# The first modulation and the LRU input in sixteen blocks of features, with fp32 products and a ring of 17 weight places

## What is computed

```python
c_act = silu(c)
mod = c_act @ w_ada + b_ada                      # 6 * 2048 columns
shift1, scale1, gate1, shift2, scale2, gate2 = split(mod, 6)
h = rms_norm(x, norm1_g) * (1 + scale1) + shift1
proj = h @ w_in                                  # 10752 columns
lru_x, lru_gate, q, k, v, g_a, g_b = split(proj)
xc = causal_depthwise_conv(lru_x, conv_w, conv_b)    # 4 taps along the sequence
# r, i = sigmoid(xc @ 128x128 blocks); rec = scan along the sequence of (a, u)
# y_a = (rec * gelu(lru_gate)) @ w_lru_out; y_b = attention(q, k, v) @ w_attn_out
```

## Time and profile before

| what | us |
|---|---|
| median of 3 runs (2783.32 to 2784.49) | 2783.36 |
| the profiled execution, its time | 2785.63 |
| its span | 2783.8 |
| TensorE busy in the span | 2671.4 (96%) |
| VectorE busy | 1963.2 (71%) |
| ScalarE busy | 1458.5 (52%) |

### The profile page before, as it was taken

The page is one execution under the profiler, slowest core; times in us unless marked ns, Lnnn a source line. Parts: engine busy times, 40 slices in busy tenths (PEclk is TensorE's granted clock), DMA queues, the critical chain, the costliest instruction groups (busy, mean ns, idle before and its releaser), DMA issues.

```text
span 2783.8 us, 40811 instructions
## 1 busy us (share of the span) xinstructions
PE 2671.4 (96%) x16090; PEld 2356.3 (85%) x16090; DVE 1963.2 (71%) x2783; ACT 1458.5 (52%) x2183; POOL 141.1 (5%) x177
## 2 busy tenths in 40 slices
PE   4789899999999999999999999999999999999996
PEld 4778788888888788888888888888988888889885
DVE  7985788887898866666566676666566766664666
ACT  3356666655545555555555545545555455445543
POOL 0000000000001000000000010100001221000002
PEclk8899999999999999999999999999999999999998
DMA  8965677778889775655566555665545556655452
GB/s 331 376 223 166 200 243 253 261 262 280 289 303 328 255 251 183 187 192 190 187 183 197 188 178 166 189 178 175 158 148 187 187 173 183 181 182 155 144 178 102
DMA packets 162110, 584.12 MB, mean 210 GB/s; under 512 B 19040, under 2 KB 20320, under 8 KB 161792
## 3 DMA queue, kind: packets, MB, share of 16 engines
q1 hardware_dynamic: 157104, 566.86, 62.7%
q0 software_dynamic: 4528, 12.43, 1.6%
q10 hardware_dynamic: 288, 2.23, 0.2%
HBM read 574.05 MB, written 2.15 MB: 207 GB/s over the span
## 4 chain that ended last, share of the span: by engine, by line
PE 86%; DVE 10%; ACT 2%; issue 1%; DMA 0%; SPq 0%; ACTq 0%; DVEq 0%
PE bank L726 49%; PE bank L734 25%; DVE raw L1408 3%; DVE wlo L1367 3%; PE bank L699 2%; PE bank L701 2%; PE bank L700 2%; PE pO L783 1%; PE pS L760 1%; PE pT L772 1%; DVE XC L1824 1%; PE pS L813 1%; ACT whi L977 1%; DMA CR<-in_c 0%; DVE bank L1810 0%
## 5 line engine op out<-in xcount | busy, mean ns | idle before, releaser
L1367 DVE TENSOR_TENSOR wlo<-raw,whi 128x1024 fp32r<-128x1024 f32 (+1 forms) x880 | 1075.2, 1234 | 460.4 <-ACT whi L977 456.7
L977 ACT ACTIVATE whi<-raw 128x1024 fp32r<-128x1024 f32 (+1 forms) x880 | 912.2, 1048 | 446.4 <-PE bank L734 355.2
L726 PE MATMUL bank<-H,whi 128*128 128x512 f32 x4000 | 1020.6, 397 | 4.7 <-DVE H L1675 3.7
L726 PEld LDWEIGHTS bank<-H,whi 128*128 128x128 f32 x4000 | 723.8, 190 | 147.0 <-issue 6.3
L734 PEld LDWEIGHTS bank<-H,wlo 128*128 128x128 f32 x4000 | 547.7, 191 | 43.4 <-DVE wlo L1367 4.1
L734 PE MATMUL bank<-H,wlo 128*128 128x256 f32 x4000 | 560.2, 283 | 2.1 <-DVE wlo L1367 2.1
L726 PE MATMUL bank<-F,whi 128*128 128x512 f32 x1024 | 256.4, 392 | 0.0
L1408 DVE SCALAR_TENSOR_TENSOR raw<-raw,CR 128x1024 f32<-128x1024 f32 x192 | 230.7, 1217 | 0.0
L726 PEld LDWEIGHTS bank<-F,whi 128*128 128x128 f32 x1024 | 184.3, 189 | 32.8
L1197 ACT ACTIVATE ET<-bank 128x512 f32<-128x512 f32 x116 | 69.1, 596 | 193.8 <-PE bank L734 193.8
L1810 DVE TENSOR_TENSOR bank<-bank,ET 128x512 f32<-128x512 f32 x116 | 80.9, 698 | 96.2 <-ACT ET L1197 96.2
(11 more groups left out here) (305 smaller groups left out, 2955.7 us busy)
## 6 DMA issues: line engine op xcount, KB each, us to landing
raw<-in_w_in SPq DMA_DIRECT2D x424, 512.0 KB, 4.2
raw<-in_w_ff SPq DMA_DIRECT2D x256, 512.0 KB, 4.3
raw<-in_ada SPq DMA_DIRECT2D x192, 512.0 KB, 5.2
raw<-in_w_out SPq DMA_DIRECT2D x96, 512.0 KB, 4.7
raw<-in_w_lru_out SPq DMA_DIRECT2D x32, 512.0 KB, 4.6
raw<-in_w_attn_out SPq DMA_DIRECT2D x32, 512.0 KB, 4.9
raw<-in_w_kv SPq DMA_DIRECT2D x32, 512.0 KB, 4.6
BT<-gtab POOLq DMA_DIRECT2D x32, 128.0 KB, 4.3
```

The source lines that it names most:

```text
L726: pe.matmul(out[i].rearrange("p (a s) -> p a s", a=2), whi[:, s, at_:at_ + 128], both[:, :, kt, :], start=(c == 0 and k == 0), stop=False, ...
L977: act.activation(whi[:, s, 0:el.n], raw[el.slot][:, 0:el.n], ACT.Copy).then_inc(s_hi, 1)
L1367: dve.tensor_tensor(wlo[:, s, 0:n], raw[el.slot][:, 0:n], v32(whi[:, s, 0:n]), ALU.subtract).then_inc(s_lo, 1)
```

## The change

- The LRU stage goes block by block of the input features: 16 steps b, each with the four ada chunks of its own 128 columns of scale1 and shift1 and two weight chunks. A weight chunk ("w32") is now one block of input features by 1024 output columns and isn't split: TensorE multiplies it as fp32, straight from `raw`, by the fp32 `XR` block (`products_plain`, 8 matmuls of 256 columns); the place comes free when TensorE is done with it. Half 0 goes to banks 0 to 3, half 1 to banks 4 to 7.
- ScalarE modulates in place once for each block; H in its two parts, which later units need, is made of four blocks at a time (one copy on ScalarE, one subtraction on VectorE, `low1`).
- The ring has 17 places in this stage (0 to 4 and 6 to 17; eight new ones lie where AT and XC come later). The last two weight chunks are bound to places 6 to 9, the next ones to 0 to 4.
- The convolutions run behind the last products: two at once, the other six as side work (`convs`), one each two ticks, spread over unit q0 to q2. Gates begin after q2, two sets go beside unit q4, and the last two beside k.
- `c` comes in two loads from two queues, x in four pieces behind c, the constants and `vec`; most of `decay` is put off to step b = 6.

```diff
-NRAW = 10
+NRAW = 18
...
-    for q in range(4):
-        mark("norm1", q)
-        for j in range(8):
-            unit("lrux", j, "in", j, "H1", nkc=1, corder=(q,), part=("open", "more", "more", "close")[q])
-            if (q, j) == (3, 0):
-                steps.append(("ring", (0, 1, 2, 3, 4)))
+    for b in range(NB):
+        mark("norm1", b)
+        for half in range(2):
+            unit("lrux", half, "x", half, "H1", nkc=1, corder=(b,), part="open" if b == 0 else "close" if b == NB - 1 else "more")
     mark("lru_weights")
     for j in range(8):
-        unit("q", j, "in", 8 + j, "H1")
-        if j == 0:
+        unit("q", j, "in", j, "H1")
+        if j == 2:
             mark("bias")
-        if j < 7:
-            mark("gates", j)
-        if j == 6:
-            mark("gates", 7)
-    unit("k", 0, "in", 16, "H1")
+            mark("gates", 0)
+        elif j == 3:
+            mark("gates", 1)
+            mark("gates", 2)
+        elif j > 3:
+            mark("gates", j - 1)
+    mark("gates", 7)
+    unit("k", 0, "in", 8, "H1")
     mark("scan")
-    unit("v", 0, "in", 17, "H1", mode="t")
+    unit("v", 0, "in", 9, "H1", mode="t")
...
...
     first_end = []
...
+    def columns(block):
+        for half in range(2):
+            modulation(block, half)
...
-        stream.append(Elem("w", 4 * un.width, (un.src, un.u, un.kc0 + un.corder[c]), ord=len(order) - 1))
...
+        stream.append(Elem("w32" if un.part else "w", CH if un.part else 4 * un.width, (un.src, un.u, un.kc0 + un.corder[c]),
+                           ord=len(order) - 1))
...
+    columns(16)
+    columns(0)
+    first_end.append(len(stream) - 1)
+    for b in range(1, NB):
+        weight(parts[2 * b - 2], 0)
+        columns(16 + b)
+        weight(parts[2 * b - 1], 0)
+        columns(b)
+        first_end.append(len(stream) - 1)
+    rings.append((len(stream), (6, 7, 8, 9)))
+    weight(parts[-2], 0)
+    weight(parts[-1], 0)
+    rings.append((len(stream), (0, 1, 2, 3, 4)))
...
+        if el.kind == "w32":
+            done.append(("chunk", el.ord + 1))
+            continue
...
-            un.bank = un.j
+            un.bank = 4 * un.j
...
-        if un.part in ("", "close"):
+        if un.part == "close" and un.j == 0:
+            holder = {0: ("lrux", 2), 1: ("lrux", 4)}
...
+    raw += [at(f"raw{10 + i}", [128, CH], o_a + i * 4096) for i in range(8)]
...
-        sp.dma_start(vec[:, :], d_vec).then_inc(s_vec, 16)
-        for h in range(2):
-            sp.dma_start(CR[h][:, :], d_c[:, h * CH:(h + 1) * CH]).then_inc(s_c, 16)
+        sp.dma_start(CR[0][:, :], d_c[:, 0:CH]).then_inc(s_c, 16)
...
+        def products_plain(un):
+            ch = un.chunks[0]
+            el = stream[order[ch]]
+            kt = un.corder[0]
+            pe.wait_ge(s_hf, kt + 1)
+            pe.wait_ge(s_raw[el.slot], el.landed)
+            for k in range(8):
+                ins = pe.matmul(banks[un.bank + k // 2][:, k % 2 * 256:k % 2 * 256 + 256], raw[el.slot][:, k * 128:(k + 1) * 128],
+                                XR[:, kt, :], start=(un.part == "open" and k % 2 == 0), stop=(un.part == "close" and k % 2 == 1),
+                                skip_group_check=True)
+            ins.then_inc(s_mm, 1)
...
+                elif un.kind == "q" and un.j == 0:
+                    pe.wait_ge(*ready["H1"](kt))
...
-                act.activation(Hhi[:, b, :], XR[:, b, :], ACT.Identity, scale=A1v[:, b:b + 1],
-                               bias=mod[:, b:b + 1]).then_inc(s_hh, 1)
-                if b >= 4:
-                    act.wait_ge(s_h, b - 3)
-                act.activation(tslot(b), XR[:, b, :], ACT.Identity, scale=A1v[:, b:b + 1],
-                               bias=mod[:, b:b + 1]).then_inc(s_slp, 1)
+        def norm1(b):
+            act.wait_ge(s_mod, b + 1)
+            act.wait_ge(s_xr, b // 2 + 1)
+            act.activation(XR[:, b, :], XR[:, b, :], ACT.Identity, scale=A1v[:, b:b + 1], bias=mod[:, b:b + 1]).then_inc(s_hf, 1)
+            if b % 4 == 3:
+                act.wait_ge(s_hf, b + 1)
+                act.activation(Hhi[:, b - 3:b + 1, :], XR[:, b - 3:b + 1, :], ACT.Copy).then_inc(s_hh, 4)
...
+        def conv(j):
+            if j == 0:
+                for r in range(14, 18):
+                    act.wait_ge(*last_use[r])
+            act.wait_ge(s_mm, first_split - 1 + j // 4)
+            for i in range(2):
+                b = 2 * j + i
+                ins = act.activation(XC[:, b, :], banks[j][:, i * 256:(i + 1) * 256], ACT.Identity, scale=v(V_CW + 48 + b),
+                                     bias=v(V_CB + b))
+            ins.then_inc(s_pre, 1)
+        def convs():
+            conv(2)
+            yield
+            for j in range(3, 8):
+                conv(j)
+                yield from ticks(2)
...
+            if kind == "q":
+                if j == 0:
+                    for r in range(10, 14):
+                        act.wait_ge(*last_use[r])
...
+        act.dma_start(CR[1][:, :], d_c[:, CH:2 * CH]).then_inc(s_c, 16)
         act.dma_start(cst[:, 0:C_DUP], d_cst[:, 0:C_DUP]).then_inc(s_cst, 16)
-        act.dma_start(RES[:, :, :], d_x).then_inc(s_x, 16)
+        act.dma_start(vec[:, :], d_vec).then_inc(s_vec, 16)
+        for q in range(4):
+            act.dma_start(RES[:, 4 * q:4 * q + 4, :], d_x[:, 4 * q:4 * q + 4, :]).then_inc(s_x[q], 16)
...
-        act.wait_ge(s_x, 16)
         for j in range(8):
+            act.wait_ge(s_x[j // 2], 16)
...
-                    side.start(gates(st[2], 3 if st[2] == 7 else 1))
...
-            evac(un)
+            if un.part:
+                if un.j == 0:
+                    conv(0)
+                    conv(1)
+                else:
+                    side.start(convs())
+            else:
+                evac(un)
...
-        def first_columns(q):
-            sums(first_end[q])
-            both = [slice(16 + 4 * q, 20 + 4 * q), slice(4 * q, 4 * q + 4)]
-            for c in both:
-                t = vc.add(dve.tensor_tensor(mod[:, c], mod[:, c], mod2[:, c], ALU.add))
+        def first_columns(b):
+            sums(first_end[b])
+            for c in (16 + b, b):
+                t = vc.add(dve.scalar_tensor_tensor(out=mod[:, c:c + 1], in0=mod[:, c:c + 1], scalar=mod2[:, c:c + 1],
+                                                    in1=v(V_ADA + c), op0=ALU.add, op1=ALU.add))
             dve.wait_ge(s_vc, t)
-            for c in both:
-                t = vc.add(dve.tensor_tensor(mod[:, c], mod[:, c], vec[:, V_ADA + c.start:V_ADA + c.stop], ALU.add))
-            dve.wait_ge(s_vc, t)
-            dve.scalar_tensor_tensor(out=A1v[:, 4 * q:4 * q + 4], in0=mod[:, both[0]], scalar=1.0, in1=v(V_N1 + 4 * q, 4),
+            dve.scalar_tensor_tensor(out=A1v[:, b:b + 1], in0=mod[:, 16 + b:17 + b], scalar=1.0, in1=v(V_N1 + b),
                                      op0=ALU.add, op1=ALU.mult).then_inc(s_mod, 1)
...
+                if el.kind == "w32":
+                    continue
...
-        def scaled(q):
-            for j in (2 * q, 2 * q + 1):
-                dve.tensor_tensor(XR[:, 2 * j:2 * j + 2, :], RES[:, 2 * j:2 * j + 2, :], over(Rv, 2), ALU.mult).then_inc(s_xr, 1)
-        def norm1(q):
-            for b in range(4 * q, 4 * q + 4):
-                dve.wait_ge(s_hh, b + 1)
-                dve.wait_ge(s_slp, b + 1)
-                dve.tensor_tensor(Hlo[:, b, :], tslot(b), v32(Hhi[:, b, :]), ALU.subtract).then_inc(s_h, 1)
-            if q < 3:
-                scaled(q + 1)
+        def scaled(j):
+            dve.tensor_tensor(XR[:, 2 * j:2 * j + 2, :], RES[:, 2 * j:2 * j + 2, :], over(Rv, 2), ALU.mult).then_inc(s_xr, 1)
+        def norm1(b):
+            if b % 2 == 0 and b < 14:
+                scaled(b // 2 + 1)
+            if b % 4 == 1 and b > 4:
+                low1(b // 4 - 1)
+            if b == 6:
+                decay()
+        def low1(q):
+            sl = slice(4 * q, 4 * q + 4)
+            dve.wait_ge(s_hh, 4 * q + 4)
+            dve.tensor_tensor(Hlo[:, sl, :], XR[:, sl, :], v32(Hhi[:, sl, :]), ALU.subtract).then_inc(s_h, 4)
...
+        def conv(j):
+            dve.wait_ge(s_pre, j + 1)
+            for i in range(2):
...
-        dve.wait_ge(s_vec, 16)
-        decay()
         for h in range(2):
             dve.wait_ge(s_ct, h + 1)
             dve.scalar_tensor_tensor(out=CR[h][:, :], in0=CT[:, h, :], scalar=1.0, in1=CR[h][:, :], op0=ALU.add,
                                      op1=ALU.mult).then_inc(s_cr, 1)
         dve.wait_ge(s_cr, 2)
-        feed(6)
+        dve.wait_ge(s_vec, 16)
+        decay_begin()
+        feed(first_end[1] - 1)
         root(-1, EPS, False)
-        feed(8)
+        feed(first_end[1])
         newton(-1, R4)
         dve.wait_ge(s_rv, 1)
         scaled(0)
-        feed(first_end[0])
...
-            evac(un)
+            if un.part:
+                if un.j == 0:
+                    low1(3)
+                    conv(0)
+                    conv(1)
+                else:
```

(56 more changed lines are left out.)

82 lines of the change are left out of this document (29 added, 53 removed).

## The result

The changed kernel takes 2765.0 us (median of four runs, 2763.1 to 2768.5) against 2783.3 for the kernel before: a ratio of 0.9936, 95% interval 0.9924 to 0.9949, 18.3 us less where 22 were forecast. Five more runs beside the experiments gave 2767.7 and 0.9941 (0.9928 to 0.9953), 15.0 us less than the kernel before beside them (2782.7). The profiled execution took 2768.5 us, the slowest of its four, and its own gain is 17.1.

A forecast was written before the change was run, and what follows sets the result against it. TensorE bounds the kernel except where it waits, as in the LRU stage, bound by VectorE. Gain 174.9 - 152.6 + 2.9 - 2.9 = 22.3, rounded to 22, giving 2761.4 us; range 2751 to 2775, own range 2755 to 2771.

The forecast's parts named there:

- What bounds the stage: LRU stage before the change: VectorE is the bound, its ada sums and subtractions busy 75.1 and 41.0 us.
- The start: Head of the LRU stage: first sum near 10, TensorE starts its products at 31.0 us against 48.41; bounds 29 to 36.
- The products: LRU products: 256 fp32 matmuls at 0.43 us, 110.1 us, 6.9 per step; 2.9 us lost to the clock.
- The transfers: LRU stage loads: 7.7 us a step at 410 GB/s, data ahead of TensorE at every step.
- by a nose: LRU stage: TensorE itself is narrowly the bound, reaching the last step at 137.1 against data at 133.8.
- The 17 places cover this: LRU stage ring: a weight chunk's place, reused 21.8 us later, is free in time, with margin growing 0.8 each step.
- The end of the stage: Last LRU chunks to q0: late chunk lands 140.8, then splits and convolutions; q0 begins at 152.6 instead of 174.91.
- Behind it: From q0 on: 2.9 us saved on convolutions cancels 2.9 lost to the clock; gates cost nothing, bounds -1 to 4.
- Rival (1): LRU stage: transfers are the bound at 350 GB/s, q0 near 166, gain 9, time 2774; chance 0.12.
- Rival (2): Behind the LRU stage: convolutions, gates and table loads collide, TensorE waits 6 to 10 us more, time 2769; chance 0.12.
- Rival (3): LRU stage: TensorE doesn't get full clock, products cost 0.86 us each, 2868 at worst; chance 0.04.
- Rival (4): LRU stage ring: stuck ada chunk, 17 places act as fewer, at most 12 us, time 2773; chance 0.05.

The follow-up runs named there:

- b_start: The kernel before with only the change's new start (c in two loads first on two queues, x in four pieces, decay later): 2782.3 us, ratio 0.9996.
- e_start: The changed kernel with VectorE's root and newton put behind five of the first sums, not seven and eight: 2766.2 us, ratio 0.9933.
- e_ring9: The changed kernel with the old ring of nine places in the LRU stage: 2774.5 us, ratio 0.9964.
- e_conv: The changed kernel with the first two convolutions ahead of the splitting of q's first two chunks: 2762.3 us, ratio 0.9921.
- e_half: The changed kernel with half of the fp32 products of steps 1 to 14 left out, all transfers kept: 2762.3 us, ratio 0.9925.
- after_again: The changed kernel once more, unedited, five runs beside the experiments: 2767.7 us, ratio 0.9941.
- e_last: The changed kernel with the last two weight chunks of the LRU stage in places 10 and 11, not 6 and 7: 2762.9 us, ratio 0.9928.
- e_gates: The changed kernel with all eight gate sets done by unit q7, none beside k: 2759.5 us, ratio 0.9917.
- after: The changed kernel's first profile, no edit: median of four runs 2765.0 us, ratio 0.9936; the profiled execution took 2768.5 us.

## Why the prediction was right, and where it was off

*What bounds the stage.* Right: VectorE before. b_start shows it again: with it still the bound, 5 us at its head, 3.4 of them its own work put off, are worth 1.

*The start.* 31.0 forecast (its terms add up to 30.8), 32.24 measured, by the route that was named: first sum at 10.13, root behind the seventh sum. VectorE's seventh sum and its root:

```profile
24.16 1.23 DVE L1461 SCALAR_TENSOR_TENSOR raw<-raw,CR 128x1024 f32<-128x1024 f32 x1 [1.33 <-DMA raw<-in_ada]
...
25.31 0.42 DVE L1475 TENSOR_SCALAR BT<-pS 128x256 f32<-128x256 f32 x1
```

The seventh sum was to be done near 24.1 and was at 25.3, as its chunk wasn't there before 24.16. From there on all took 6.9 us, as forecast. So the 1.2 us are the transfers', and x, whose last pieces were squared from 20.6, held nothing up.

*The products.* 0.43 us each, 6.91 for a step, both as worked out from the gates' rows; none of them waits for its weights. The loss by the clock was nearly as charged (2.9): the first step takes 9.4 us (32.24 to 41.69), 2.5 more than 6.9.

*The transfers.* Here a step failed that hid itself in the sum. I had TensorE as the bound "by a nose", data 3.3 us ahead at the last step. They were behind: the timeline has step 14 from 131.5, so TensorE was free for step 15 at 138.4, and H came at 138.6 (138.01 + 0.6). I had H of step 15 at 133.8 (by my own terms, 16.5 + 7.7 x 15 + 2.4, it is 134.4). Of the 4.2 to 4.8 us it came later, 1.2 are those of the start, and 2.2 are those of 30 to 50, where transfers ran at 355 and 373 GB/s, not 410 (55/410 and 37/410 of 10 us each), behind places that TensorE held (409 in e_start, 18 in e_ring9); about 1 us is left that I can't place. "The 17 places cover this" was 2 us too kind. That it cost only 0.3 us is luck: the 3.3 us of lead that I had counted took up the rest. The same stage in e_conv, with a slower step 0, has TensorE as the bound (step 15 at 139.00, without a wait). Which of the two is the bound decides what more would pay: less work for TensorE gives 1 us at most (e_half), a better fed ring 2. On the rate itself, rows decide: 407 to 413 GB/s from 50 to 120. The Trainium skill's limit of some 358 from HBM for each core ("DMA: Bandwidth & Descriptors", Specifications) isn't borne out by these stretches, with this one core at work.

*The end of the stage.* The chain was as predicted, link by link: the chunk bound to place 7, 3.7 us for its way, two splits, `low1(3)`, two convolutions. 152.6 forecast, 154.21 measured; the 1.6 are those that step 15 was late by. In after_again step 15 begins at 138.76 and q0 at 155.09, as q's second chunk was there 0.9 us later for ScalarE. e_last and e_conv each cut the chain and moved q0 by 3.9 and 4.6 us.

*Behind it.* The two losses that I set against each other did cancel: q0 to v took 118.2 us before and 118.5 after; q0's first two chunks lost 2.8 to the clock (2.9 charged), and no convolution holds up q0 to q2. The term that was mis-sized is the gates: "nothing", with 4 as its bound, and it was 3.3. I had counted ScalarE's and VectorE's free time over 20 us of q units and not over unit k, where two sets, k's evacuation and the scan's first table load and root fall together on ScalarE. e_gates gives it back whole.

*Sum.* 22.3 - 1.6 (q0 late) - 0.3 (q0 to v) - 3.3 (gates) = 17.1, the profiled gain at ya and at the end. The median gained 18.3. 2765.0 lies in the range and in the forecast's own range. The gain of 22 was too high by 3.7 us for one median and by 7 for the other (15.0). Rival (1) said that transfers are the bound, and at step 15 they were, by 0.3 us; its reason, a rate near 350, and its time were not borne out. Rival (2) is what happened at half its least size. Rival (3), the clock, had no part in the stage behind step 0. Rival (4) appears with nine places, 5.8 us at q0, and its reason in the changed kernel too, in the 2.2 us of 30 to 50.

## What to carry to other kernels

When a change takes a stage off one engine, work out the next two limits to the same us, and ask of a ring who holds its places while the slower of the two hasn't begun. A load bound to a place that is only a few loads old is a wait in disguise, and everything behind it in its queue inherits it. Side work that is pushed back must find its time in the very unit where it lands, beside that unit's evacuation, not in an average over many.

## What the runs showed of the hardware

The spread of the changed kernel's runs (2760.7 to 2768.5 us) has a likely cause in how soon the clock comes back, and two places show it.

The first is step 0. Five profiles have the same program up to step 15's loads (after, after_again, e_gates, e_conv and e_last). TensorE begins between 32.14 and 32.42 in all, and its first sixteen records take 6.16, 6.00, 5.28, 6.73 and 5.86 us. Step 15 begins at 137.82 in the one with 5.28 and at 139.00 in the one with 6.73.

The second is the norm near 920 us, where TensorE waits the same 2.71 us in two kernels that do the same there. The changed kernel (timeline of TensorE, then two stretches):

```profile
923.29 1.19 PE L755 MATMUL bank<-H,whi 128*128 128x512 f32 x4 [2.71 <-DVE H L1736]
...
924.00:928.00 4.00, 2.90 (x13) 2.36 (x12) 3.17 (x6) 4.00 (x7) 0.00 (x0) 0.58 0.60 195
...
932.00:936.00 4.00, 4.00 (x17) 3.53 (x16) 2.46 (x3) 1.39 (x3) 0.00 (x0) 0.64 0.98 355
```

and e_gates, which is there 4.4 us earlier:

```profile
918.86 1.50 PE L760 MATMUL bank<-H,whi 128*128 128x512 f32 x4 [2.71 <-DVE H L1741]
...
920.00:924.00 4.00, 3.42 (x13) 2.53 (x12) 3.18 (x6) 4.00 (x6) 0.00 (x0) 0.63 0.54 201
...
928.00:932.00 4.00, 4.00 (x23) 3.43 (x22) 2.01 (x4) 2.33 (x5) 0.00 (x0) 1.00 1.01 313
```

Behind the same wait the clock falls in both, to 0.58 and 0.63. Some 9 us behind the wait it is at 1.00 in e_gates and at 0.64 on average in the changed kernel, and e_gates gains 2.3 us there (21.6 to 23.9 from ya to the MLP), and by the last stage 5 us in all. The second profile of the changed kernel, of a run of 2768.4 us, shows what the first does (0.57, and 0.65 in 932 to 936); of its quicker runs none has a profile. That several such waits fall out by chance would explain runs of one kernel that lie 3 to 8 us apart; this is argued, not shown. The Trainium skill ("TensorE: Matmul & The Clock Gate", HAM clock gate) says that the number of slow products at a start varies from run to run; the rows of step 0 agree.

One kind of fall was not expected: 3.0 us of idle time were enough, and the clock fell 1 to 2 us after TensorE was at work again (e_conv). Being back at full clock did not keep the fall off there.
